# One chain of steps for all head pairs in prompt attention, and another order of retention's first loads

## The reference, cut to what matters

```python
def sb_attend(q, k, v, qpos, kpos, bias):
    z = jnp.einsum('bqhd,bkhd->bhqk', q, k) * scale + bias
    log_keep = jnp.where(mask, jax.nn.log_sigmoid(-z), 0.0)
    log_between = lax.cumsum(log_keep, axis=3, reverse=True) - log_keep
    w = jnp.where(mask, jnp.exp(jax.nn.log_sigmoid(z) + log_between), 0.0)
    return jnp.einsum('bhqk,bkhd->bqhd', w, v)
```

## Time and profile before

| | us |
|---|---|
| three runs of before | 2085.12, 2087.53 (median), 2088.31 |
| the profiled execution | 2085.59 |
| its span, first to last instruction | 2083.8 |
| prompt attention, first transpose to last `finish` | 437.8 to 698.9 |
| attention of the samples | 702.7 to 825.8 |
| retention | 1652.1 to 2083.8 |

### The profile page before, as it was taken

How to read it: one execution, slowest core, us unless ns; L and a number is a source line. 1 busy time by engine, 2 the same in 40 slices (tenths; PEclk the granted TensorE clock), 3 DMA queues, 4 the chain that set the end, 5 groups by cost and what they waited for, 6 DMA issues and landing times. The chain is left out here.

```text
span 2083.8 us, 31335 instructions
## 1 busy us (share of the span) xinstructions
PE 1893.4 (91%) x11538; PEld 1518.7 (73%) x11538; DVE 860.5 (41%) x1480; ACT 522.4 (25%) x1133; POOL 596.6 (29%) x532
## 2 busy tenths in 40 slices
PE   6999999967787787596999999999999879999998
PEld 5788998944454454474889998888888747777776
DVE  4551000047787445783444442111000245656564
ACT  5210110145665433242420000000111223323231
POOL 3332222025565201513043222222331142212130
PEclk9999999978988898698999999999999979999999
DMA  4233232152243264615533323222224377665643
GB/s 150 88 104 109 90 110 91 48 166 73 70 120 101 72 195 144 211 65 176 173 115 95 94 84 109 89 86 86 91 93 143 121 196 221 202 191 167 210 137 137
DMA packets 210238, 261.57 MB, mean 126 GB/s; under 512 B 24260, under 2 KB 150916, under 8 KB 209860
## 3 DMA queue, kind: packets, MB, share of 16 engines
q1 hardware_dynamic: 154436, 199.53, 31.1%
q10 hardware_dynamic: 53680, 55.14, 8.1%
q0 software_dynamic: 2000, 5.25, 0.8%
HBM read 176.10 MB, written 81.40 MB: 124 GB/s over the span
## 5 line engine op out<-in xcount | busy, mean ns | idle before, releaser
L440 PE MATMUL odd_bank<-odd_w_hi,odd_h_hi 128*128 128x512 f32 x576 | 224.1, 389 | 0.0
L440 PE MATMUL odd_bank<-odd_w_lo,odd_h_hi 128*128 128x512 f32 x576 | 224.1, 389 | 0.0
L440 PE MATMUL odd_bank<-odd_w_hi,odd_h_lo 128*128 128x512 f32 x512 | 199.2, 389 | 0.0
L388 POOL CAST odd_w_hi<-ahead_raw 128x1024 fp32r<-128x1024 f32 x48 | 51.4, 1071 | 334.5 <-PE odd_bank L440 312.7
L440 PE MATMUL odd_bank<-odd_h_hi,odd_w_hi 128*128 128x362 f32 (+1 forms) x384 | 126.7, 330 | 1.8 <-POOL odd_w_lo L390 1.8
L440 PE MATMUL odd_bank<-odd_h_lo,odd_w_hi 128*128 128x362 f32 (+1 forms) x384 | 126.7, 330 | 0.0
L440 PE MATMUL even_bank<-even_h_hi,even_w_lo 128*128 128x362 f32 (+1 forms) x384 | 126.0, 328 | 0.0
L440 PE MATMUL even_bank<-even_h_hi,even_w_hi 128*128 128x362 f32 (+1 forms) x384 | 125.9, 328 | 0.0
L440 PE MATMUL even_bank<-even_h_lo,even_w_hi 128*128 128x362 f32 (+1 forms) x384 | 125.8, 328 | 0.0
L440 PE MATMUL odd_bank<-odd_h_hi,odd_w_lo 128*128 128x362 f32 (+1 forms) x384 | 125.6, 327 | 0.0
L440 PEld LDWEIGHTS odd_bank<-odd_w_hi,odd_h_hi 128*128 128x128 f32 x576 | 108.1, 188 | 22.5
(11 more groups left out here) (333 smaller groups left out, 4083.4 us busy)
## 6 DMA issues: line engine op xcount, KB each, us to landing
ahead_raw<-in_w_in_odd SPq DMA_DIRECT2D x48, 512.0 KB, 3.9
even_raw<-in_w_in_even SPq DMA_DIRECT2D x32, 512.0 KB, 3.8
k_page<-in_cache_k SPq DMA_DIRECT2D x64, 256.0 KB, 3.1
v_page<-in_cache_v SPq DMA_DIRECT2D x64, 256.0 KB, 3.1
rt_s<-in_state_ret SPq DMA_DIRECT2D x32, 512.0 KB, 5.2
v_tm<-odd_shared ACTq DMA_DIRECT2D x64, 128.0 KB, 2.0
g_tm<-odd_shared ACTq DMA_DIRECT2D x64, 128.0 KB, 1.9
ahead_place<-v_tm SPq DMA_DIRECT2D x32, 256.0 KB, 5.2
```

The source lines that it names most:

```text
L388: nc.gpsimd.tensor_copy(hi, r).then_inc(w_hi_done, 1)
L440: mm = pe.matmul(out, stationary, moving, start=(j == 0), stop=(j == len(pairs) - 1))
```

## The change

Prompt attention: `steps` now lists the steps of all four pairs (96 in one chain), and every engine's program is written out for all of them, with no hardware loop; `NS2` is 48 bodies. The q and k of pair p+1 are transposed within pair p, one group of four transposes at the end of bodies 3, 4, 6 and 8, into the output bank `o[1]`, which is free until the first half of the queries opens it in body 10; the hi and lo parts exist twice, v is loaded in place twice, and the bias is read in place. Constants, gate, `w` and the second v lie where the second page buffer of values is, so the 16 loads of pages of that buffer move from prompt attention to the start of attend_samples. SyncE stores the result. In retention SyncE's first loads are put in another order: `s0` and `g` of step 0 after the wait for the stage before, `raw` after the loads of step 3, `y` one by one in steps 1 to 7 (one in each, `y[n-1]` in step n, after that step's store and state loads) and the gates of the second four samples in step 2. No arithmetic changes.

```diff
+        NPAIR = HA // 2
...
+        later, at, spot = pages.v[1][:].rearrange("p u n -> p (u n)"), 0, []
+        for n in (P, P, P, 8 * P, TP, NW * NQ):
+            spot.append(later[:, at:at + n])
...
-        steps = [(e, half, kb, lo) for half, kb, lo in head_steps for e in range(2)]
-        NSTEP = len(steps)
-        NS2 = NSTEP // 2
+        steps = [(p, e, half, kb, lo) for p in range(NPAIR) for half, kb, lo in head_steps for e in range(2)]
+        NSTEP = 2 * len(head_steps)
+        NS2 = len(steps) // 2
...
+        turns_at = {NSTEP // 2 * p + k: (p + 1, i) for p in range(NPAIR - 1) for i, k in enumerate((3, 4, 6, 8))}
...
+        def turn_bank(p, i):
+
+            return (o[1] if p else z[i])[:].rearrange("p (c n) -> p c n", n=P)
...
+            load_qk(0)
+            load_v(0)
+            load_v(1)
             for p in range(NPAIR):
...
+                if p + 1 < NPAIR:
+                    sp.wait_ge(turned, 4 * p + 4)
+                    load_qk(p + 1)
+                if p:
+                    store_mix(p - 1)
+                    sp.wait_ge(mix_left, 16 * p)
+                sp.dma_start(gate[:], gate_fm[pair_cols(p), 0:TP]).then_inc(gate_load, 16)
+                if 1 <= p < NPAIR - 1:
+                    sp.wait_ge(pv_done, NSTEP * p)
+                    load_v(p + 1)
                 if p == 0:
                     pages.load_table(sp)
-                pages.load(sp, p % 2, keys=p < 2)
...
+                if p < NPAIR - 1:
+                    pages.load(sp, p % 2, keys=p < 2)
+            store_mix(NPAIR - 1)
...
+            def turn(p, i):
+                pe.wait_ge(qk_load, 32 * p + 32)
+                if p:
+                    pe.wait_ge(mixed, 4 * (p - 1))
+                    pe.wait_ge(turn_read, 4 * p + i)
...
+            for k in range(-1, NS2 + 2):
...
+                        if half == 0 and p + 1 < NPAIR:
+                            pe.wait_ge(turn_read, 4 * (p + 1) + 4)
...
+                if k in turns_at:
+                    turn(*turns_at[k])
...
+            for k in range(NS2 + 2):
+                if k >= 2:
+                    weigh(2 * k - 4)
+                    weigh(2 * k - 3)
+                if k < NS2:
+                    softplus(2 * k)
+                if k - 1 in turns_at:
+                    round_turned(*turns_at[k - 1])
+                if k < NS2:
+                    softplus(2 * k + 1)
...
+            for k in range(-1, NS2 + 3):
+                for e in range(2):
+                    if 0 <= k < NS2:
+                        drop(2 * k + e)
+                    if k + 1 < NS2:
+                        cap(2 * (k + 1) + e)
+                    if e == 0 and k - 1 in turns_at:
+                        split_turned(*turns_at[k - 1])
+                for j in (2 * k - 6, 2 * k - 5):
+                    if j >= 0 and closes[j]:
+                        finish(j)
@@ -1327,6 +1353,7 @@
             for dst, name in ((sel, "as_sel"), (own, "as_own")):
                 sp.dma_start(dst[:], consts[name]).then_inc(const_in, 16)
             sp.dma_start(gate[:], gate_fm[:, TP:T].rearrange("(c p) t -> p c t", p=P)).then_inc(const_in, 16)
+            pages.load(sp, 1, keys=False)
             first.load(sp)
             for n in range(NS // 2):
                 i = n % 2
@@ -2212,13 +2239,11 @@
                 sp.wait_ge(s1_done, J * (m + 1))
                 sp.dma_start(state_samples[c, h].rearrange("(j k) v -> k j v", k=P), s1[m % 2]).then_inc(s1_left[m % 2], 16)
 
-            load_s0(0)
-            load_g(0)
             for x in ahead.left_tm:
                 sp.wait_ge(x, LEFT)
-            load_raw(0)
+            load_g(0)
+            load_s0(0)
             load_g(1)
-            load_s0(1)
             for n in range(NSTEP):
                 h, c = divmod(n, NCH)
                 if n + NQ < NSTEP:
@@ -2229,13 +2254,11 @@
                     sp.wait_ge(v_split, n + 1)
                     load_v(n + NV)
                     if n == 0:
+                        load_raw(0)
                         load_g(2)
-                        load_s0(2)
-                        load_s0(3)
-                        load_y(0)
+                        for x in range(1, SEQS):
+                            load_s0(x)
                         load_gs(0, 0)
-                        load_y(1)
-                        load_gs(0, 1)
                     sp.wait_ge(gated, unit_of["step", n] + 1)
                     load_g(n + NV)
                 if c == NCH - 1:
@@ -2247,11 +2270,13 @@
                         sp.wait_ge(o_done, unit_of["samples", (n - 1) // SEQS] + 1)
                         for x in (n + 2, n + 3) if (n - 1) % SEQS == 1 else (n + 3,):
                             load_s0(x)
-                if n < NCH - 3:
-                    if n == 1:
+                if 1 <= n < NCH:
+                    if n == 4:
                         sp.wait_ge(w_split_d, R // 2)
                         sp.wait_ge(w_split_p, R // 2)
-                    load_y(n + 2)
+                    load_y(n - 1)
+                if n == 2:
+                    load_gs(0, 1)
                 if n == NCH - 1:
                     for seq in range(NS):
                         sp.wait_ge(stacked[seq], NSTACK)
```

More of the change, by code:

```diff
@@ new lines, in _ @@
+            for g, (_, _, _, _, lo) in enumerate(steps):
+                m = g % ND
+                pool.wait_ge(carry_done, g + 1)
+                if g >= ND - 2:
+                    pool.wait_ge(summed, g - ND + 3)
+                nc.gpsimd.tensor_copy(k_hi[:, m, lo:NQ], sums[:, g % NX, lo:NQ]).then_inc(carry_hi, 1)
+                pool.wait_ge(carry_hi, g + 1)
+                nc.gpsimd.tensor_tensor(k_lo[:, m, lo:NQ], sums[:, g % NX, lo:NQ], k_hi[:, m, lo:NQ].bitcast(F32),
+                                        ALU.subtract).then_inc(carry_split, 1)
@@ L1096, in _ @@
         @block.tensor
         def _(pe):
-            pe.sem_inc(turned, 1)
-            pe.sem_inc(pv_done, 1)
-            pe.sem_inc(summed, 1)
+            def turn(p, i):
[3 more added lines that the diff above has]
+                    pe.wait_ge(turn_read, 4 * p + i)
+                for c in range(4):
+                    mm = pe.transpose(turn_bank(p, i)[:, c, :], qk_in[:, i // 2, 4 * (i % 2) + c, :], ident[:])
+                mm.then_inc(turned, 1)
@@ new lines, in round_turned, with weigh @@
+            def round_turned(p, i):
+                act.wait_ge(turned, 4 * p + i + 1)
+                if p >= 2:
+                    act.wait_ge(logits, NSTEP * (p - 1))
+                nc.scalar.activation(turned_to(qk_hi, p, i), turn_bank(p, i), ACT.Copy,
+                                     scale=DA ** -0.5 if i < 2 else 1.0).then_inc(turn_hi, 1)
+            def weigh(j):
+                p, e, _, _, lo = steps[j]
+                act.wait_ge(summed, j + 1)
+                if j >= NW:
+                    act.wait_ge(pv_done, j - NW + 1)
+                nc.scalar.activation(w[:, j % NW, lo:NQ], z[j % NZ][:, lo:NQ], ACT.Exp,
+                                     bias=biases[:, 2 * p + e:2 * p + e + 1]).then_inc(w_done, 1)
@@ new lines, in softplus @@
+            def softplus(i):
+                at = sums[:, i % NX, steps[i][4]:NQ]
+                act.wait_ge(capped, i + 1)
+                nc.scalar.activation(at, at, ACT.Exp).then_inc(exp_done, 1)
+                act.wait_ge(exp_done, i + 1)
+                nc.scalar.activation(at, at, ACT.Ln, bias=1.0).then_inc(soft_done, 1)
+            for i in range(4):
+                round_turned(0, i)
+            for k in range(NS2 + 2):
[8 more added lines that the diff above has]
+                    softplus(2 * k + 1)
@@ new lines, in split_turned, with cap @@
+            def split_turned(p, i):
+                hi = turned_to(qk_hi, p, i).bitcast(F32)
+                dve.wait_ge(turn_hi, 4 * p + i + 1)
+                dve.scalar_tensor_tensor(turned_to(qk_lo, p, i), turn_bank(p, i), DA ** -0.5 if i < 2 else 1.0, hi,
+                                         ALU.mult, ALU.subtract).then_inc(turn_read, 1)
+            def cap(i):
+                p, e, _, _, lo = steps[i]
+                dve.wait_ge(logits, i + 1)
+                if i >= NX:
+                    dve.wait_ge(carry_split, i - NX + 1)
+                if i >= NX - 2:
+                    dve.wait_ge(carry_done, i - NX + 3)
+                dve.tensor_scalar(sums[:, i % NX, lo:NQ], z[i % NZ][:, lo:NQ], biases[:, 2 * p + e:2 * p + e + 1], CAP,
+                                  ALU.add, ALU.min).then_inc(capped, 1)
@@ new lines, in finish @@
+            def finish(j):
+                p, e, half, _, _ = steps[j]
+                rows = slice(DA * e, DA * e + DA)
+                cols = slice(half * NQ, half * NQ + NQ)
+                dve.wait_ge(pv_done, j + 1)
+                if run[j] == 0:
+                    dve.wait_ge(gate_load, 16 * p + 16)
```

(3 more changed lines are left out.)

254 lines of the change are left out of this document (83 added, 171 removed).

## The result

The changed kernel takes 2050.75 us in the median of 4 runs (2047.05 to 2054.25), the kernel before 2086.32 in the same comparison (2081.68 to 2088.31): ratio 0.9828, 95% interval 0.981 to 0.9846. The prediction was 2054.4 (2042 to 2068). The profiled executions are 2085.59 and 2047.05, spans 2083.8 and 2044.8: 39.0 us less. The trace divides them: retention's first scores start at 1624.75 instead of 1652.33, 27.6 earlier, all of it prompt attention's (the samples' first GpSimd instruction is already 27.5 earlier, at 675.13), and from those scores to the end 11.4 are gained. Predicted were 20.7 and 12.4.

The account below looks back on a forecast made before the run. In prompt attention no engine is full: VectorE limits wide bodies, latency narrow ones; retention waits for a load of k. 2085.6 - 20.7 - 12.4 = 2052.5, plus 1.9: 2054.4 us, range 2042 to 2068.

Parts of the forecast that it names:

- The boundary, body 11 to body 3, 17.0: Prompt attention, one pair's body 11 to the next's body 3: 17.0 us, like the boundary of halves, where it was 26.3.
- Body 7 to 11, 17.2: Prompt attention, narrow bodies 7 to 11: 16.86 us, plus 0.2 for the split and 0.1 for two caps, 17.2.
- Wide bodies, 22.0: Prompt attention, bodies 3 to 7, four 512-wide steps: 22.0 us, with VectorE's own floor at 21.8.
- Turning, 2.2 a pair: Prompt attention, preparing the next pair's q and k: three VectorE low parts in full bodies cost 2.0 us, the fourth 0.2.
- Sum of a pair, 58.2: Prompt attention, period of a pair: 58.2 us against 65.10, saving 6.9 at each of three boundaries, 20.7 in all.
- the 55 under which the prediction called itself wrong: Prompt attention: the prediction is wrong if a pair takes over 62 us or under 55.
- Rival 4: Prompt attention: TensorE's clock falls within the chain; at 0.60 a pair takes 75 us and the kernel 2115; chance 0.02.
- First pair and end of stage, 0 within 1: Prompt attention: the first pair's start, the last drain and the last store stay, 0, within 1 us each way.
- Moved page loads, 0: Start of the samples' attention: 16 loads of the second value buffer move there; price 0, without cover 17 us of queue.
- Retention, 9.0 for k and 3.4 for the clock: Retention's start: no wait for step 4's k saves 9.0 us, TensorE staying at full clock 3.4 more; sum 12.4.
- Stacking wait stays at 5.84: Retention's start: TensorE's 5.84 us wait for small stacking DMAs stays; up to 9 more if fewer loads land them early.
- k to land between 1666 and 1681, asked for at 1682: Retention: step 4's k lands at 1666 by the early rate, 1681 in proportion; TensorE asks for it at 1681.9.

Follow-up runs that it names:

- pool_unrolled: The kernel before with GpSimd's prompt-stage loop over the pairs written out and the empty semaphore increment before its cast removed; ratio 0.999 (0.9978 to 1.0001).
- chain_alone: The changed kernel's chained prompt attention with retention's loads in the order of the kernel before; ratio to the kernel before 0.9883 (0.9862 to 0.9903).
- together_split: Changed kernel with VectorE's two adds together, last in wide bodies, and two sample states and gates loaded behind step 4's q, k, v; ratio to before 0.9956.
- add_late: The changed kernel with VectorE capping the next body's step before the carry's add, in every body; ratio to the kernel before 0.9823 (0.9807 to 0.9839).
- stack_hold: The changed kernel with SyncE waiting for the first stacking copies before loading three sample states and gates in retention; ratio to the kernel before 0.9853.
- s0_late: The changed kernel with retention's loads of three sample states and gates moved behind step 4's g, without a wait; ratio to the kernel before 0.9846.

## Why the prediction was right, and where it was not

- *The boundary, body 11 to body 3, 17.0:* 16.7. Right, and for the reason given: the seam of pairs is that of halves (17.1 with the increment put back).
- *Body 7 to 11, 17.2:* 16.7. 0.4 went with the increment (16.9 before, 16.4 in `pool_unrolled`; 17.1 and 16.7 in the chain), which the prediction did not have, and its added 0.3 did appear against those 16.4. But the split is not in it, since without the turning it is also 16.7; the last pair, behind which no caps follow, takes 16.5.
- *Wide bodies, 22.0, "VectorE is the limit", floor 21.8:* wrong reason and 1.2 too much. The 2.73 a step was an alternation of GpSimd and VectorE; its add of 1.36 held 0.67 of waiting, counted as busy time. I overlooked an instruction in the diff, the increment that GpSimd loses, worth 0.14 a step, 1.1 for eight.
- *Turning, 2.2 a pair:* 0.1. The failed step is "three of them stand in bodies where VectorE has no idle time". It had 0.55 a step of it, hidden in the add.
- *Sum of a pair, 58.2:* 54.2 undisturbed, below the 55 under which the prediction called itself wrong; in after's trace 56.5, 57.0, 53.9, in the mean 55.8. With the increment put back the least disturbed period takes 56.2, so of the 4.0 by which the forecast was too high about 2.0 are the increment's and the rest is the turning that cost nothing. Of the 12 us of unforeseen gain (three times 4.0) 4.8 are given back in the disturbances, which the sum had not: one or two stretches at half clock in the midst of the chain. In after the wide bodies of pair 1 took 22.39, the clock being 0.73 and 0.59 from 515 to 525, and body 11 to 3 of pairs 1/2 took 19.12, the clock being 0.50 from 560 to 570. Rival 4 named this; its size is 2.4 to 5 us an execution, not 60. The gain of the stage, 27.6, lies outside the predicted 14 to 26.
- *First pair and end of stage, 0 within 1:* pair 0 gave 0.9 (499.26 against 498.33), the end cost 1.0 (last low part 28.5 earlier, the samples 27.5). Right.
- *Moved page loads, 0:* the stages between the samples' start and retention's kept their length to 0.1. Right. v for pair 2 was loaded at 513, 40 us before use.
- *Retention, 9.0 for k and 3.4 for the clock:* 9.0 and 3.4. Right. *Stacking wait stays at 5.84:* it became 7.3, and 0.5 of those 1.5 came back in the products behind it: 9.0 + 3.4 - 1.5 + 0.5 = 11.4. The 1.5 need be no effect of the change: with the loads in the order of before the wait was 5.84, 6.93 (`pool_unrolled`) and 7.38 (`chain_alone`), in the order of after 5.35 to 7.75 in eight traces. So no effect of the 1.75 MB less in SyncE's queue shows, as the prediction took from the Trainium skill ("DMA: Bandwidth & Descriptors", queues, rings and completion order). In the two runs in which that queue ran low the copies came early. Whether it has to be empty for that stays open: with one sample state left in it (`together_split`) the wait was 2.57.
- *k to land between 1666 and 1681, asked for at 1682:* even the slow bound was too early, and there is no margin. Counted from the first scores, that bound is 28.5 us and k is asked for after some 30. In after k landed 14.8 us after its issue at 1638.86, that is after 28.9, and waited 1.6 for its use, helped by a stacking wait that was longer by 1.5; in the seven other traces with the same order of loads it landed after 30.3 to 32.4. That the whole 9.0 was saved is therefore part luck. In four of these runs k was 2.0 (twice), 3.9 and 4.0 late, as here without the turning:

```profile
1655.92 0.71 PE L2361 MATMUL rt_sckt<-ahead_place 128*128 128x128 f32 x4 [3.96 <-DMA ahead_place<-k_fm]
```

In these the projection came 39.9 to 40.5 after the first scores, in the other four 35.1 to 35.8: against the 46.6 of before a gain of about 6 or about 11, where 12.4 was predicted (6 to 21). A miss of 2 costs 5: in `add_late` the scores of step 4 are 1.9 later than in after, and from them to the projection it is 8.1 again instead of 4.7 (granted clock 0.57 from 1655 to 1660, in after 1.00). That would fit the spread of after's runs (7 us) and the smaller median gain, 35.6 against 38.5 in the profiled pair; with one trace a kernel this is argued, not shown.

Together: too little by 7 in the prompt stage, too much by 1 in retention, against the profiled execution; that the total came within 4 us of the median is partly luck. Undisturbed, three periods would have gained 12 more than forecast; falls of the clock took 4.8 of it, and the median pair gained 3 less than the profiled one.

## What to carry to other kernels

A busy engine in a profile may be waiting inside its instructions: compare the duration of the same shape in different places (0.69 and 1.25 here) before calling it full, and look at what another engine does at that moment. In a cycle between two engines count each instruction between a wait and its work, an empty increment too. Where the DMA engines are full, another order of loads mostly moved the wait here; it gained only until the first thing that was needed landed just in time, and then a small miss cost the clock as well.

## What the runs showed of the hardware

- A low part on GpSimd and an add with two SBUF inputs on VectorE exclude each other in both directions. VectorE's add goes from 0.69 to 1.25; with both casts first, GpSimd's low part took 1.73 when the add had come first (517.56), and a cast beside an add 1.00 in place of 0.61. Instructions of VectorE whose tile inputs are not both in SBUF (drop, cap, split) kept 0.74 and 0.68 beside it.
- A semaphore increment by itself in GpSimd's program: 0.14 us.
- TensorE's clock fell in work without long gaps. Windows of the chained prompt stage in `chain_alone`:

```profile
588.00:605.00 17.00, 14.56 (x89) 9.30 (x86) 13.75 (x27) 11.55 (x26) 10.73 (x17) 1.00 0.00 1
605.00:610.00 5.00, 2.77 (x13) 1.61 (x11) 2.17 (x6) 3.27 (x8) 3.13 (x7) 0.76 0.00 0
610.00:615.00 5.00, 4.45 (x16) 2.19 (x15) 2.20 (x5) 2.08 (x5) 2.09 (x4) 0.50 0.00 0
615.00:620.00 5.00, 4.34 (x20) 3.22 (x20) 4.36 (x8) 2.26 (x6) 3.00 (x4) 0.50 0.00 0
620.00:625.00 5.00, 4.46 (x18) 2.54 (x14) 4.40 (x6) 2.60 (x6) 2.56 (x4) 0.53 0.56 209
```

  It granted 1.2 GHz from about 608 to 625 at the boundary of pairs 2 and 3, and 2.4 through the boundaries of pairs 0/1 and 1/2, which have the same instructions. In the window of the fall TensorE was busy for 2.77 of 5 us, its longest gap 1.36. At the same boundary of after it was busy for as long, and the clock held:

```profile
610.00:615.00 5.00, 2.77 (x13) 1.56 (x13) 2.81 (x6) 2.26 (x6) 3.91 (x7) 1.00 0.00 0
```

  There it fell at the boundary of pairs 1 and 2, and so it did in `stack_hold` and `s0_late`, whose prompt stage is the same; but that of `chain_alone` is the same too. Why it falls at one boundary and not at another stays open.
- Stacking copies of 32 KB issued by GpSimd landed 11.3 us after their issue beside a full queue (the last of the first three, issued at 1636.4 in after; TensorE's use at 1647.86) and 5.6 beside one that was held back (the same copy in `stack_hold`, issued at 1640.4).
